# Product-key experts: scores per quarter of the query, two tiles ranked by pairs of heads, 112 of 256 sums kept

## What is computed

```python
q = (xt @ w_pq).reshape(T, 8, 2, 128)                # 8 heads, two halves
s1 = einsum('thd,hnd->thn', q[:, :, 0], k1)          # 128 scores per half
s2 = einsum('thd,hnd->thn', q[:, :, 1], k2)
t1, i1 = top_k(s1, 16);  t2, i2 = top_k(s2, 16)
cand = t1[..., :, None] + t2[..., None, :]           # 16 x 16 = 256 sums
ts, ci = top_k(cand, 16)
e = take(i1, ci // 16) * 128 + take(i2, ci % 16)     # expert numbers
g = softmax(ts)
out = sum_k g * gelu(xt . u_tab[e]) * v_tab[e]       # then x += out
```

## Time and profile before

| what | value |
|---|---|
| median of 3 runs | 2625.52 us (2622.42 to 2629.32) |
| the profiled execution | 2618.87 us |
| its span in the trace | 2617.1 us |
| busy share of the span: PE, DVE, ACT, POOL | 90%, 60%, 25%, 37% |
| query, from 976 to 1081 us | 105 us |
| scores, to 1101 us | 20 us |
| up stage with ranks and hot stage, to 1913 us | 812 us |
| change of stage, to 1953 us | 40 us |
| down stage, to the end | 664 us |

### The profile page before, as it was taken

One profiled execution on the slowest core, in us unless ns is written; L12 is line 12 of the kernel. 1 busy time (PEld: TensorE's weight loads), 2 busy tenths in 40 slices (PEclk: granted clock), 3 DMA queues, 4 the chain that ended last, 5 costly groups with the idle time before them and its releaser, 6 DMA issues.

```text
span 2617.1 us, 29396 instructions
## 1 busy us (share of the span) xinstructions
PE 2349.2 (90%) x11005; PEld 1803.2 (69%) x11005; DVE 1576.7 (60%) x2535; ACT 664.3 (25%) x1404; POOL 972.9 (37%) x552
## 2 busy tenths in 40 slices
PE   6799999899789999998888888877779999999996
PEld 6699977655468879998888888877744444444442
DVE  2376654444632330199898889999935555555555
ACT  2244420123412311333333333433310000100001
POOL 8454554400014234166755566444411111111110
PEclk9799999855799999999999998899889999999998
DMA  6323233200133122157666567677699999999994
GB/s 234 108 97 109 92 129 113 89 16 17 43 95 141 49 81 94 58 179 251 223 215 214 191 223 254 233 274 270 226 335 373 379 385 377 376 380 383 386 384 176
DMA packets 191825, 539.83 MB, mean 206 GB/s; under 512 B 16977, under 2 KB 116114, under 8 KB 158290
## 3 DMA queue, kind: packets, MB, share of 16 engines
q1 hardware_dynamic: 113024, 243.30, 27.1%
q0 software_dynamic: 27776, 201.40, 20.0%
q10 hardware_dynamic: 50898, 93.43, 10.0%
HBM read 471.13 MB, written 66.62 MB: 205 GB/s over the span
## 4 chain that ended last, share of the span: by engine, by line
PE 65%; DVE 22%; issue 4%; POOL 3%; DMA 2%; ACT 2%; SPq 1%; ACTq 0%; POOLq 0%; DVEq 0%
PE ps L919 23%; PE ps L554 18%; PE ps L874 9%; PE ps L671 4%; DVE yg L1837 4%; DVE hot L1955 3%; PE ps L704 3%; PE ps L533 2%; DVE hot L1957 2%; DVE ring L1829 2%; PE ps L754 1%; DMA ge<-ge_scratch 1%; PE ps L708 1%; DVE hot L1959 1%; POOL wL L470 1%
## 5 line engine op out<-in xcount | busy, mean ns | idle before, releaser
L919 PE MATMUL ps<-vraw,gf 128*128 128x512 f32 x1536 | 664.2, 595 | 17.6 <-DVE gf L1971 10.7
L919 PEld LDWEIGHTS ps<-vraw,gf 128*128 128x128 f32 x1536 | 292.7, 191 | 388.5 <-issue 373.4
L484 POOL DMA_INDIRECT ring<-uv,place_of x192 | 229.7, 1196 | 794.6 <-DVE yg L1837 787.0
L874 PE MATMUL ps<-actH,uH 128*128 128x384 f32 x1024 | 364.0, 355 | 67.2 <-POOL uL L476 64.6
L476 POOL TENSOR_TENSOR uL<-uraw,uH 128x1024 fp32r<-128x1024 f32 x128 | 339.5, 2669 | 159.2 <-ACT uH L1339 158.4
L466 POOL TENSOR_SCALAR wH<-raw 128x1024 fp32r<-128x1024 f32 x112 | 120.5, 1094 | 641.6 <-PE ps L554 488.5
L874 PE MATMUL ps<-actL,uH 128*128 128x384 f32 x1024 | 356.2, 348 | 0.0
L874 PE MATMUL ps<-actH,uL 128*128 128x384 f32 x1024 | 355.0, 347 | 0.0
L1837 DVE SCALAR_TENSOR_TENSOR yg<-ring,coef,yg 128x1024 f32<-128x1024 f32 x192 | 291.2, 1516 | 41.6 <-ACT coef L1390 41.5
L554 PE MATMUL ps<-actH,wH 128*128 128x288 f32 (+1 forms) x960 | 287.0, 299 | 7.0 <-DVE actL L1493 7.0
L554 PE MATMUL ps<-actH,wL 128*128 128x288 f32 (+1 forms) x960 | 285.2, 297 | 0.0
(11 more groups left out here) (246 smaller groups left out, 3257.3 us busy)
## 6 DMA issues: line engine op xcount, KB each, us to landing
uraw<-wu SPq DMA_DIRECT2D x128, 512.0 KB, 4.2
vraw<-wv SPq DMA_DIRECT2D x128, 512.0 KB, 7.9
raw<-wts SPq DMA_DIRECT2D x56, 1024.0 KB, 4.9
ge_scratch<-ge ACTq DMA_DIRECT2D x128, 192.0 KB, 4.0
c_scratch<-cst ACTq DMA_DIRECT2D x12, 2048.0 KB, 8.3
cg<-c_scratch SPq DMA_DIRECT2D x32, 768.0 KB, 9.7
ge<-ge_scratch SPq DMA_DIRECT2D x128, 192.0 KB, 8.3
xres<-x ACTq DMA_DIRECT2D x2, 2048.0 KB, 12.0
```

The costliest lines, as they stand in the source:

```text
L484: pool.indirect_dma_start(out=ring[:, s % RING, :], out_offset=None, in_=a["uv"], in_offset=bass.IndirectOffsetOnAxis(ap=place_of[:, s:s + ...
L874: mm = pe.matmul(bank(b, TD), lhs, rhs, start=k == 0 and w == 0, stop=k == KT - 1 and w == 2)
L919: mm = pe.matmul(bank(2 * i + half), gf[:, q % GF_RING, i * P:(i + 1) * P], vraw[:, q % V_RING, half * CHUNK:(half + 1) * CHUNK], start=q ...
```

## The change

- **Scores by quarter.** Each of the four query chunks holds two heads, which is 4 of the 16 lists. Their scores are made behind the third group of the next chunk (the last ones behind the whole query), for the tiles in the order 4, 0, 1, 2, 3, into the rotating PSUM banks. `pqT` holds two chunks instead of four. The scores of tile 3 go through DRAM and are loaded again behind `high(2)`; `score_ready` is gone.
- **Two tiles by pairs of heads.** `rank` gets a first head and a number of heads. Tile 4 and tile 0 are ranked two heads at a time, in the order (4,0) (0,0) (4,1) (0,1) (4,2) (4,3), then tile 4's picks, then (0,2) (0,3), then tile 4's gates. No gathered steps lie between. Tiles 1, 2 and 3 are ranked whole, with eight steps each.
- **112 of 256 sums.** The best 16 sums of two sorted lists lie among the pairs (x, y) with x < 4 or y < 4. Two additions make 4 x 16 and 12 x 4 sums; row and column are found from the place by eleven small operations instead of five.
- **Other places.** The first step's slot, the ranks, the transposes and the hot stage come earlier in n; the hot stage reaches from n = 75 to 127. Steps 24 to 63 (40 of them) lie in it. POOL stops at n = 5 for the picks and at n = 13 for the gates. The gain of the last norm is loaded in the down stage, with the residual.

The diff, cut to its core:

```diff
-EXP4_AT, EXPD_AT, TURN_AT, EXP3_AT, HOT_AT, HOT_TO = 14, 77, 82, 100, 96, 126
+PICKS_AT, GATES_AT, EXP4_AT, EXPD_AT, TURN_AT, EXP3_AT, HOT_AT, HOT_TO = 5, 13, 5, 54, 60, 78, 75, 127
 RANK_STEPS = 8
+RANKED = 3 * RANK_STEPS
+EARLY_STEPS = 64
+WIDE, NARROW = 4, 4
+GRID = WIDE * TOPK + (TOPK - WIDE) * NARROW
+def hot_of_step(s):
+    return (s - RANKED) * HOTS // (EARLY_STEPS - RANKED)
 def step_place(s):
-    if s < 4 * RANK_STEPS:
-        return 14 + int(2.5 * (s + 1))
-    return hot_place(min(HOTS - 1, hot_of_step(s))) // 2
+    if s < RANKED:
+        return 12 + int(2.5 * (s + 1))
+    return hot_place(hot_of_step(s)) // 2 if s < EARLY_STEPS else 2 * NKEYS
...
-            if n == EXP4_AT + 2:
+            if n == PICKS_AT:
                 pool.wait_ge(picks_ready, 1)
                 two_halves(place_of, eu)
-                pool.wait_ge(gates_ready, 1)
-                two_halves(gates_of, chosen[:, DENSE, 2, :])
-                pool.wait_ge(picks_in, 64)
+            if n == PICKS_AT + 1:
+                pool.wait_ge(ssb_ready, N_PQ * TILES)
+                pool.wait_ge(picks_in, 32)
                 for s in range(RING):
                     gather(s)
                 issued = RING
-            while RING <= issued < STEPS4 and step_place(issued - RING) + 4 <= n:
+            if n == GATES_AT:
+                pool.wait_ge(gates_ready, 1)
+                two_halves(gates_of, chosen[:, DENSE, 2, :])
+            while issued >= RING and step_place(issued - RING) + 4 <= n:
                 gather(issued)
                 issued += 1
...
+        def scores_of(c):
+            b, value = queries[c]
+            pe.wait_ge(emptied[b], value + 1)
+            if c == 0:
+                pe.wait_ge(keys_in, 16)
+            for i in SCORED:
+                b, value = turns.take()
+                pe.wait_ge(emptied[b], value)
+                for s in range(4):
+                    mm = pe.matmul(ps[0:ROWS[i], b * BANK + s * P:b * BANK + (s + 1) * P],
+                                   pqT[:, c % 2, s, T0[i]:T0[i] + ROWS[i]], keys[:, 4 * c + s, :], start=True, stop=True)
+                mm.then_inc(filled[b], 1)
...
+        def copy_scores(c):
+            for i in SCORED:
+                b, _ = wait_filled()
+                four = slice(4 * c, 4 * c + 4)
+                if i == DENSE:
+                    if c >= 2:
+                        act.wait_ge(ss_store[c % 2], 16 * (c // 2))
+                    dst = stage[:, c % 2]
+                else:
+                    dst = ssb[i][0:ROWS[i], four]
+                act.activation(dst, bank(b, CHUNK, ROWS[i]).rearrange("p (s n) -> p s n", s=4), ACT.Copy)\
                    .then_inc(emptied[b], 1)
+                act.wait_ge(emptied[b], _ + 1)
+                act.sem_inc(ssb_ready, 1)
+                if i == DENSE:
+                    act.dma_start(ss_d[:, four, :], stage[:, c % 2]).then_inc(ss_store[c % 2], 16)
...
+        copy_scores(N_PQ - 1)
         high(2)
+        for j in range(2):
+            act.wait_ge(ss_store[j], 16 * N_PQ // 2)
+        act.dma_start(ssb[DENSE][:, :, :], ss_d).then_inc(ss_in, 16)
...
+            step.done(ve.tensor_copy(p, besti[0:rows]))
+            ve.tensor_scalar(whole, p, 1.0 / TOPK, -0.5 * (TOPK - 1) / TOPK, ALU.mult, ALU.add)
+            step.done(ve.tensor_scalar(other, p, 1.0 / NARROW, -0.5 * (NARROW - 1) / NARROW, ALU.mult, ALU.add))
+            ve.tensor_scalar(whole, whole, ROUND, None, ALU.add)
+            step.done(ve.tensor_scalar(other, other, ROUND, None, ALU.add))
+            ve.tensor_scalar(whole, whole, -ROUND, None, ALU.add)
+            step.done(ve.tensor_scalar(other, other, -ROUND, float(WIDE - WIDE * TOPK // NARROW), ALU.add, ALU.add))
+            step.done(ve.tensor_tensor(whole, whole, other, ALU.max))
+            ve.scalar_tensor_tensor(place, whole, -float(TOPK), p, ALU.mult, ALU.add)
+            step.done(ve.scalar_tensor_tensor(other, whole, -float(NARROW), p, ALU.mult, ALU.add))
+            step.done(ve.scalar_tensor_tensor(place, other, -float(WIDE * TOPK - WIDE * NARROW), place, ALU.add, ALU.max))
...
-        rank(4, nothing)
+        for i, c in ((4, 0), (0, 0), (4, 1), (0, 1), (4, 2), (4, 3)):
+            rank_pair(i, c)
         expert_places(4, eu[0:NS_TOK, :])
         ve.sem_inc(picks_ready, 1)
+        for c in (2, 3):
+            rank_pair(0, c)
...
-        for i in range(DENSE):
-            rank(i, gathered)
+        ve.wait_ge(ssb_ready, N_PQ * TILES)
+        for i in range(1, DENSE):
+            rank(i, 0, PK_HEADS, full_work, gathered)
```

More of the change, by code:

```diff
@@ L560, in chunk, with feature_chunk @@
             release[0] = 1
-        def feature_chunk(slot, n_tok, n_parts):
+        def feature_chunk(slot, n_tok, n_parts, after=None):
             def make(blk, part):
@@ L571, in make @@
                 return (lambda b: bank(b, n_tok)), terms
-            chunk(slot, [make(blk, part) for blk in range(4) for part in range(n_parts)])
+            chunk(slot, [make(blk, part) for blk in range(4) for part in range(n_parts)], after)
         def token_group(slot, i, rows, t0):
@@ L1850, in nothing, with rank @@
             pass
-        def rank(i, between):
+        def rank(i, first, n, work, between):
             rows, at = ROWS[i], min(i, DENSE)
-            best_of(S2, ssb[i], top, topi, rows)
+            pick, top, topi, topf, best, besti, bestf = work
+            mine = slice(first * TOPK, (first + n) * TOPK)
+            best_of(2 * n, ssb[i][:, 2 * first:2 * (first + n), :], top, topi, rows)
             between()
@@ L1864, in rank @@
+            step.done(ins)
             between()
[L1865 removed]
+            best_of(n, sums, best, besti, rows)
             between()
             between()
[L1869 to L1873 removed]
@@ L1874, in rank @@
-            step.done(ve.tensor_scalar(whole, whole, -ROUND, None, ALU.add))
-            step.done(ve.scalar_tensor_tensor(place, whole, -float(TOPK), place, ALU.mult, ALU.add))
+            whole, place = bestf[0:rows, 0], bestf[0:rows, 1]
+            other = pick[0:rows, 0:n * TOPK].rearrange("p (h t) -> p h t", t=TOPK)
+            p = pick[0:rows, n * TOPK:2 * n * TOPK].rearrange("p (h t) -> p h t", t=TOPK)
+            step.done(ve.tensor_copy(p, besti[0:rows]))
+            ve.tensor_scalar(whole, p, 1.0 / TOPK, -0.5 * (TOPK - 1) / TOPK, ALU.mult, ALU.add)
@@ L1886, in rank @@
             indices = topf[0:rows].rearrange("p (h r) j -> p h r j", r=2)
-            long = [rows, SLOTS, TOPK]
+            long = [rows, n * TOPK, TOPK]
+            cube = [rows, n, TOPK, TOPK]
             for half in range(2):
@@ L1939, in gathered_and_gates @@
             gathered()
-        rank(DENSE, gathered_and_gates)
+        ve.wait_ge(ss_in, 16)
+        rank(DENSE, 0, PK_HEADS, full_work, gathered_and_gates)
         expert_places(3, place_of[:, STEPS4:STEPS])
@@ L1960, in _ @@
                              chosenT[:, 2, now].unsqueeze(2).broadcast_to(shape), ALU.mult).then_inc(hot_ready, 1)
-            while steps[0] < STEPS4 and hot_of_step(steps[0]) <= g:
+            while steps[0] < EARLY_STEPS and hot_of_step(steps[0]) <= g:
                 gathered()
@@ L1976, in _ @@
             weigh(q)
-            gathered()
+            if steps[0] < STEPS:
+                gathered()
         accumulate(STEPS - 1)
```

145 lines of the change are left out of this document (74 added, 71 removed).

## The result

The changed kernel takes 2576.85 us (median; 2574.68 to 2580.62) where the kernel before takes 2625.64 in the same comparison: a ratio of 0.9823 with a 95% interval of 0.9810 to 0.9836, 48.8 us less on the medians. I had forecast 2556 (70 us less) with a range of 2518 to 2594. The direction and the order of the gain are right, the size was 21 us too hopeful. Its profiled execution took 2580.62 us, with a span of 2578.8.

A forecast was written before the change was run, and what follows sets the result against it. Bound: a ring of waits in the ranks, DVE in the hot stage. Gain 70 us: 111 from the earlier first rank, 27 from shorter ranks, less 68 in the hot stage; 2549 profiled, median 2556, range 2518 to 2594.

The forecast's parts named there:

- The ring: Full ranks: DVE, PE and POOL wait on each other, none full; a steady rank falls from 105.3 to 101.2 us.
- Rival A: Full ranks: the ring opens, a rank takes DVE's own 86 us; gain 103 us, 2522 us; chance 0.18.
- the middle stall: Steady rank, PE: 8.8 us before 1363.48 because the gather waits out the 8 lists of 256; it goes.
- Query and scores: Scores in four parts inside the query: up starts at about 1101 as before; cost 0, at most 3 us.
- Pairs: Eight two-head rankings: 14.6 us undisturbed, 15.5 in the query, 17.5 beside up; first full rank at 1154 instead of 1169.9.
- nearly free: POOL's stops at group 5 for picks and 13 for gates: added waits hardly delay the low parts PE needs.
- First full rank: First of three full ranks: starts at 1154, ends at 1242 with its group-30 coefficient, so 88 us.
- Hot stage: Stage after the ranks: 382 us (bounds 365 and 405) instead of 314, DVE setting the end at 1830.
- B: Hot stage: leaves DVE's hands, DVE losing 24 us by waiting; gain 45 us, 2581 us; chance 0.18.
- C: Hot stage: hot tiles and token matmuls alternate, 10 us a group, 480 in all; 28 us slower, 2654; chance 0.03.
- Rival E: Pairs: eleven small operations each wait out a subtraction, 38 us a pair; first full rank 98 us slower, 2723; chance 0.01.
- D: Pairs don't run beside the query; first full rank at 1245, 91 us later; 21 us slower, 2647; chance 0.02.

The follow-up runs named there:

- before: The kernel without the change, measured in the same comparison: 2625.64 us (median).
- after: The changed kernel with the whole change, against the kernel without it: 2576.85 us, ratio 0.9823.
- late-pairs run: Changed kernel, but each pair of heads ranked only once all 20 quarters of scores are there: 2654.71 us, ratio 1.0128 against the kernel without the change.

## Why the prediction was right, and where it was off

**What bounds it.** Right. The ring among DVE, POOL, ScalarE and PE was read from the earlier trace rows and predicted 101.2 us for the steady rank; 100.6 was measured. The 112 sums alone gave 100.3 in the kernel before. (The last rank of before takes 110.2 us and not 109.5; nothing hangs on it.) Rival A (86 us a rank, 2522) fell for the reason given. What I had not asked is how cheaply the ring could be opened: two groups of delay for the ranks' gathers bring a rank to 93.3, in both kernels. The rows in question are not even needed so early: in the second rank of after POOL stood 12.77 and 11.60 us at two gathers whose rows DVE took up 27 and 43 us later, with PE's next low part behind them. The GELUs of after show that the middle stall went and the other two stayed:

```profile
1299.82 0.47 ACT L1404 ACTIVATE ge<-ps 128x384 f32<-128x384 f32 x1
...
1311.02 0.49 ACT L1404 ACTIVATE ge<-ps 128x384 f32<-128x384 f32 x1 [9.22 <-PE ps L904]
...
1356.79 0.49 ACT L1404 ACTIVATE ge<-ps 128x384 f32<-128x384 f32 x1 [2.15 <-PE ps L904]
...
1369.97 0.49 ACT L1404 ACTIVATE ge<-ps 128x384 f32<-128x384 f32 x1 [10.81 <-PE ps L904]
```

From 1311.02 to 1356.79 there are eleven distances of 4.16. The stalls are 7.0 and 9.0 us; forecast were 7.3 and 10 to 11.

**Query and scores.** Up starts at the same distance from the query. The detour of tile 3's scores cost ScalarE 2.2 us of waiting for the last store; up started 0.7 us later against the query than before, so it was hidden as said. The first pair came 2.4 us later than worked out.

**Pairs.** The term that was mis-sized. Undisturbed 15.06 us against 14.6: 3.7 us over eight. Blocked time 27.8 us (148.3 us for eight pairs less 120.5) against the 13 I had put in: 15 more. The clearing, gates and fold: 11.9 us against 4, of which 8.3 are the one addition that met a burst. Off against that go 5 us of idleness between pairs that did not come, since DVE was late anyway. My upper bound (each of 27 POOL operations strikes once) gave 57 us for the pairs and held; the value inside it was taken by the average of tile 4's rank, two thirds of which are list searches (MAX8, FIND_INDEX8, MATCH_REPLACE8) that the trace never shows blocked: in after each of them on 112 or 128 elements takes 0.25 to 0.30 us. A pair has a smaller share of these and a larger one of casts and additions, and I did not draw the conclusion. Half of the 15 us arose in the first five pairs, where I had put in 0.9 us each: they lost 12.2 us, 8.6 of them in (0,0) beside the query's weight split and 3.4 in (4,2). The other half is in the last three pairs, with the cast of 9.46 us. So the sign that I had given ("over 1175: pairs above 20 us") read the wrong way: the first full rank came past 1175 with pairs of 18.5 us on average, and the passage behind them made up the rest.

**The stops of POOL.** I called them "nearly free", looking only at whether PE would run short. The text named what stands behind the stop on POOL, but not what POOL does when it is let go: it catches up in one burst, and DVE's operation stands still for it. That was worth 5.4 us, by the run with the stops moved. Nor was the stop for the gates free for PE: since DVE reached the gates late, the GELU of group 14 came 13.6 us behind that of group 13, where 4.16 would do.

**First full rank.** Mis-sized by 6.6 us. I had it end at the coefficient with the slot at group 30, which PE was to finish at 1242 with one stall of 8. The GELUs of groups 29 and 30 in after, and DVE's waits in this rank:

```profile
1270.14 0.49 ACT L1404 ACTIVATE ge<-ps 128x384 f32<-128x384 f32 x1 [13.07 <-PE ps L904]
...
1274.30 0.49 ACT L1404 ACTIVATE ge<-ps 128x384 f32<-128x384 f32 x1 [2.15 <-PE ps L904]
```

```profile
DVE yg L1887 <- ACT coef L1442: 8.9, 2, 4.6
```

Group 30 is done at 1274 (1268 with the 6 us taken off), behind three stalls of 9.4, 14.7 and 11.3 us beyond the 4.16: at the gates, at the fifth gather (19.76 us of POOL's waiting) and at the ninth (11.58). So DVE waits 8.9 us for coefficients, where I had taken PE to be ahead. It is not the lateness of the pairs: the rank takes 94.6 us too in the runs with the stops moved and with the pairs behind all scores. With the ranks' gathers two groups later the waits are gone and it takes 91.5.

**Hot stage.** Right to 2 us: 379.9 against 382, with 54 subtractions, one more than counted, at about 2.1 us each (377.6 us busy less the 169 and 94 of undisturbed work), where I had 2.19. DVE waited 0.5 us for coefficients; rivals B and C fell. That the price is POOL's and not DVE's own is shown by the run with half subtractions. The rule of the Trainium skill, "SBUF — State Buffer", section "Who interferes with whom", that an operation of either engine holds the shared pair to its end, agrees with these rows. Rival E, which took each small operation to wait out a subtraction, did not come: of the eleven small index operations of a pair none to two were struck.

**D and the other side.** The late-pairs run is D's case. It cost 80 us over after, where D had 91 over the forecast; against before it is 33 us slower, where D had 21.

## What to carry to other kernels

A queue that waits for one engine and feeds another ties the two together: move the wait as late as its data allow before speeding up either engine; here that one number was worth 36 us in the old kernel and 14 in the new one. Count such a delay in time, not in iterations, since the same "two groups later" is 8 to 10 us in the ranks and 14 to 20 in the hot stages (380/54 and 314/32 us a group), where DVE then waits for the row. And where a move puts a wait on an engine, ask what that engine does on release: the burst of caught-up work can cost another engine time (5.4 us in the trace here, too little to be told in the median). The best version tried, the changed kernel with the ranks' gathers later, takes 2558.9 us, 0.9769 of the kernel before; with the stops moved as well it can't be told from that.

## What the runs showed of the hardware

A DVE operation that meets a run of POOL's subtractions can be held to the end of the run: with four back to back (9.40 us) a cast of 0.17 us took 9.46, with four more an addition of 0.23 us took 8.54. It isn't always so. In the same trace the two additions at 1043.70 each ended behind one of two back-to-back subtractions, after 2.42 and 2.45 us. What decides between the two cases no run here shows.

Spread apart, as in the hot stage of after, a subtraction costs a DVE that is busy throughout about 2.1 us, less than the 2.4 that it takes undisturbed.

Halving the subtraction on POOL, an engine busy 37% of the span, gave 94 us. 58 of them are in the hot stage, where DVE's lengthened operations show why: an engine far from full can set the pace of another by the operations that it holds up.
